# A two-block transformer kernel on one core: the first block's two norms taken out of the products, x loaded in column pieces

## The chip, the cores and the metric

The kernel runs on one core of a Trainium2 chip. The metric is the device time of one execution in microseconds (us); 3 runs of the kernel before gave a median of 2947.12 us. The engines are named as in the profile: PE (TensorE, the matmuls), PEld (its weight loads), DVE (VectorE), ACT (ScalarE), POOL (GpSimd) and SP, which only issues transfers. Each has an instruction queue of its own that is worked off in order, and they wait for each other through semaphores.

## What is computed

Two transformer blocks on one sequence of 256 tokens with 2048 features, all in float32. The change concerns the first block, which is, cut to what matters:

```python
def rmsnorm(x, g):
    y = x * lax.rsqrt(jnp.mean(x * x, axis=-1, keepdims=True) + EPS)   # the row factor
    return y * g                                                       # the gain

h = rmsnorm(x, norm_mix)
qa, ka, va, qb, kb, vb, ga, gb = jnp.split(h @ w_in, split_points, axis=-1)
qa, ka = rope(rmsnorm(qa, a_q_norm), pos), rope(rmsnorm(ka, a_k_norm), pos)
qb, kb = rmsnorm(qb, b_q_norm), rmsnorm(kb, b_k_norm)
merged = (sigmoid(ga) * (window_attention(qa, ka, va, sink) @ w_branch_a)
          + sigmoid(gb) * (neighbourhood_attention(qb, kb, vb, rpb) @ w_branch_b))
x = x + merged @ w_out
u = rmsnorm(x, norm_ffn) @ w_up          # 2 x 5632 columns
u = depthwise_conv3(u, conv_w) + conv_b  # over tokens
gate, val = jnp.split(u, 2, axis=-1)
x = x + (silu(gate) * val) @ w_down
```

The second block (gated linear attention, spatial gating, a SwiGLU ffn, all modulated by vectors that are products with `w_mod`) has norms of its own, written with the same helpers.

## The kernel before

**Chunks.** All large products of a stage are cut into groups of 512 output columns, and a group into chunks of 512 input features. The weights of a chunk are 1 MB; SP loads them as two transfers of 512 KB into a ring of 4 slots (`load`, L444), each when the chunk 4 places before has released its slot. The stages follow one another in one numbering of chunks: projection (`proj`, 9 groups of 4 chunks), gate (8 of 4), branch (8 of 2), wout (4 of 4), up (22 of 4), down (4 of 11), and then the second block's.

**Seven products for eight.** A chunk is computed with a scheme of seven half-size products in place of eight. For this DVE forms sums of the weight quarters (`step`, L940 to L945: `step(n)` prepares chunk n + 2) and, once per norm or per input, sums of the quarters of the activations (`combine`, L973 to L978, 4 feature tiles at a time; its semaphores are called `forms_...`). PE runs the seven products twice in a chunk (L512), into PSUM banks 0 to 6. At a group's end ACT copies one of the products (`first_keep`, L1522) and DVE puts the results together (`gather`, L957 to L967).

**A norm.** `part_ss` receives sums of squares by row from ACT (`sum_squares`, L1532; for the ffn norm `squares_of_x`, L1658), POOL makes the row factor `norm_rs` of them (`rows_rstd`, L1908 to L1916), DVE multiplies x by it, 256 columns at a time (`norm_tok`, L985), PE turns the result into feature-major form (`norm_piece`, L530; a norm has 8 such pieces of two feature tiles), ACT multiplies each tile by its gain on the way out of PSUM into `act_t` (`norm_keep`, L1543), and DVE combines. PE calls `norm_ahead` in the first three chunks: pieces 0 to 3 before chunk 0, 4 and 5 before chunk 1, 6 and 7 before chunk 2.

**The start.** SP loads the upper 128 rows of x and ACT the lower ones (1 MB each); SP's first weight load waits for the latter. ACT loads the identity matrix and the gains, waits for x, squares it, issues the 21 loads of constants (L1564) and only then comes to `norm_keep`. POOL, after the row factor and chunk 0, issues two loads of `w_mod`, 8 small ones of the bias table, and the `skew` write (L1956), which lays that table out in memory with a shift for each row.

**Head work.** In the projection, the heads of a group are normed while the next group runs: DVE gathers it in the next group's chunk 0, ACT squares it, DVE reduces (`head_squares`), ACT takes the root (`head_rstd`), DVE scales it in chunk 1 (`head_first`, L1071) and, for the rotated heads, does `head_second` in chunk 2 (L1089 to L1092); PE turns two heads behind chunk 3 (L544). The turns go through bank 7, whose users take it in an order worked out beforehand (`BANK7`).

**The modulation.** The second block's modulation vectors are accumulated all along the first block, a half (512 KB of `w_mod`, loaded by POOL, L1940) at a time, on DVE (L1035), at the chunks that `HALVES` names; `SUMS_AFTER` says behind which chunk PE turns a finished sum (L554).

**Wout to up.** After wout's last group DVE adds it to x (`wout_add`, L1176), ACT squares the last 512 columns, POOL makes the factor, and the ffn norm starts as above. In up, group 2i holds gate columns and 2i + 1 value columns. Each is gathered into `up_g` or `up_v`, turned by PE after the second following chunk (L562), and convolved by ACT and DVE.

## Time and profile before

| | |
|---|---|
| three runs | 2945.26, 2947.12, 2952.03 us |
| the profiled execution | 2944.24 us, its span 2942.4 us |
| PE busy | 2858.7 us, 97% of the span |
| PEld busy | 2405.0 us, 82% |
| DVE busy | 1957.8 us, 67% |
| ACT busy | 413.7 us, 14% |
| POOL busy | 346.8 us, 12% |
| mean granted clock of TensorE | 0.993 of 2.4 GHz |
| memory traffic | 569.47 MB, 194 GB/s over the span |

The span goes from the first to the last instruction; the execution's time is somewhat longer. The busy shares are means over stages that differ, so they say which engine works most and not what a wait is worth. For that one has to see at each place which wait ended last. Times in the timeline are from the span's start.

### The profile page before, as it was taken

The numbers are of one execution on the slowest core, as the hardware profiler recorded it, in microseconds if no ns is written. First come the engines' busy times: TensorE is split into PE (matmuls) and PEld (weight loads), VectorE is DVE, ScalarE is ACT, GpSimd is POOL, SyncE is SP. The second block draws the span as 40 slices with busy tenths as digits, with TensorE's granted clock in tenths as the row PEclk, the third lists the DMA queues.
The fourth block names the chain that finished last, engine by engine and source line by source line (L and its number), as shares of the span: only waits on it lengthen the run. The fifth ranks groups of instructions, "written<-read, shape, count | busy, mean of one in ns | idle before, by whom it ended". The sixth has DMA issues, their size and how long they took to land.

```text
span 2942.4 us, 34314 instructions
## 1 busy us (share of the span) xinstructions
PE 2858.7 (97%) x13116; PEld 2405.0 (82%) x13116; DVE 1957.8 (67%) x3074; ACT 413.7 (14%) x899; POOL 346.8 (12%) x428
## 2 busy tenths in 40 slices
PE   6999999998999999999999999999799999999998
PEld 5888888887888888888884467778688888888887
DVE  4887777987988898888761003348676666555454
ACT  2221112011111111110012122331200000000000
POOL 1011221010112121210110001111011111010000
PEclk9999999999999999999999999999999999999999
DMA  7677666676666666677773444437576676555553
GB/s 229 184 254 233 191 193 195 213 247 191 210 206 201 207 207 207 207 245 243 251 235 110 135 135 137 124 120 225 162 222 214 212 213 207 171 171 164 173 176 123
DMA packets 269765, 569.47 MB, mean 194 GB/s; under 512 B 20330, under 2 KB 21240, under 8 KB 269088
## 3 DMA queue, kind: packets, MB, share of 16 engines
q1 hardware_dynamic: 235728, 456.19, 50.1%
q0 software_dynamic: 30416, 108.87, 12.0%
q10 hardware_dynamic: 3456, 2.21, 0.3%
q8 instruction: 104, 1.70, 0.2%
q14 instruction: 61, 0.50, 0.0%
HBM read 563.28 MB, written 3.92 MB: 193 GB/s over the span
## 4 chain that ended last, share of the span: by engine, by line
PE 69%; issue 17%; DVE 6%; DVEq 3%; DMA 2%; ACT 1%; ACTq 0%; POOL 0%; POOLq 0%
PE PS L512 53%; PE PS L695 7%; PE PS L705 4%; DVEq L942 1%; DVE mem L1035 1%; DVE sums L943 1%; DVE sums L940 1%; DVE sums L945 1%; PE PS L562 1%; DMA mem<-in_w_mod 1%; DVE ring L941 1%; PE PS L842 1%; PE PS L530 0%; PE PS L715 0%; PE PS L554 0%
## 5 line engine op out<-in xcount | busy, mean ns | idle before, releaser
L512 PE MATMUL PS<-sums,mem 128*128 128x256 f32 x3584 | 1066.9, 379 | 0.0
L512 PE MATMUL PS<-ring,mem 128*128 128x256 f32 x3152 | 893.6, 379 | 0.0
L512 PE MATMUL PS<-ring,act_t 128*128 128x256 f32 x2928 | 794.2, 380 | 3.6 <-DVE mem L978 2.4
L512 PEld LDWEIGHTS PS<-sums,mem 128*128 128x128 f32 x3584 | 681.7, 190 | 93.0
L512 PEld LDWEIGHTS PS<-ring,mem 128*128 128x128 f32 x3152 | 596.1, 190 | 79.5
L512 PEld LDWEIGHTS PS<-ring,act_t 128*128 128x128 f32 x2928 | 548.9, 191 | 75.2 <-DVE mem L978 3.3
L940 DVE TENSOR_TENSOR sums<-ring 128x512 f32<-128x512 f32 x380 | 277.5, 730 | 394.0 <-PE PS L512 363.6
L1035 DVE SCALAR_TENSOR_TENSOR mem<-mem,small 128x512 f32<-128x512 f32 x480 | 353.0, 756 | 36.8 <-DMA mem<-in_w_mod 7.4
L1940 POOL DMA_DIRECT2D mem<-in_w_mod x192 | 139.3, 726 | 1599.7 <-DVE mem L1035 1481.4
L943 DVE TENSOR_TENSOR sums<-sums,ring 128x512 f32<-128x512 f32 x380 | 276.7, 728 | 29.5 <-issue 1.3
L945 DVE TENSOR_TENSOR sums<-sums,ring 128x512 f32<-128x512 f32 x380 | 270.8, 713 | 30.0 <-issue 2.2
L512 PE MATMUL PS<-sums,act_t 128*128 128x256 f32 x976 | 290.3, 379 | 0.0
L941 DVE TENSOR_TENSOR ring<-ring 128x512 f32<-128x512 f32 x380 | 260.4, 685 | 0.0
L512 PEld LDWEIGHTS PS<-sums,act_t 128*128 128x128 f32 x976 | 185.7, 190 | 25.3
L705 PE MATMUL PS<-mem,ring 128*128 128x256 f32 x640 | 142.7, 382 | 0.0
L695 PE MATMUL PS<-ring,mem 128*128 128x512 f32 x320 | 139.3, 592 | 0.0
L1522 ACT COPY first_q<-PS 128x256 f32<-128x256 f32 x85 | 31.7, 373 | 756.4 <-PE PS L512 756.4
L705 PEld LDWEIGHTS PS<-mem,ring 128*128 128x128 f32 x640 | 121.7, 192 | 17.5 <-issue 1.2
L695 PEld LDWEIGHTS PS<-ring,mem 128*128 128x128 f32 x320 | 60.1, 190 | 70.9 <-issue 70.8
L1681 ACT ACTIVATE mem<-PS,small 128x256 f32<-128x256 f32 x88 | 44.9, 561 | 375.9 <-PE PS L562 375.9
L957 DVE TENSOR_TENSOR mem<-PS,first_q 128x512 f32<-128x512 f32 x85 | 58.1, 684 | 52.6 <-PE PS L512 52.0
L1277 DVE SCALAR_TENSOR_TENSOR mem<-PS,mem 128x2048 f32<-128x2048 f32 x2 | 4.6, 2291 | 124.7 <-ACT mem L1741 124.7
(242 smaller groups left out, 1631.8 us busy)
## 6 DMA issues: line engine op xcount, KB each, us to landing
ring<-in_w_in SPq DMA_DIRECT2D x240, 512.0 KB, 3.7
mem<-in_w_mod POOLq DMA_DIRECT2D x192, 512.0 KB, 4.9
ring<-in_w_up SPq DMA_DIRECT2D x176, 512.0 KB, 3.8
ring<-in_w_ffn_in SPq DMA_DIRECT2D x176, 512.0 KB, 3.7
ring<-in_w_down SPq DMA_DIRECT2D x88, 512.0 KB, 4.3
ring<-in_w_ffn_out SPq DMA_DIRECT2D x88, 512.0 KB, 3.8
ring<-in_w_out SPq DMA_DIRECT2D x64, 512.0 KB, 4.5
ring<-in_w_branch_a SPq DMA_DIRECT2D x16, 512.0 KB, 3.6
```

Source lines behind the costliest of these rows:

```text
L512: mm = pe.matmul(product(g, j), of(j, 2 * (c if part is None else part) + q), weights(j, n, q), start=lead and j in OPENS, stop=tail, skip ...
L695: mm = pe.matmul(PS[:, bank + h, :], act_[:, CK * c + k, h * P:(h + 1) * P], ring[:, n % SLOTS, k // 2, k % 2, :], start=c + k == 0, stop= ...
L705: mm = pe.matmul(PS[:, bank + f // 2, (f % 2) * T:(f % 2) * T + T], ring[:, n % SLOTS, k // 2, k % 2, f * P:(f + 1) * P], act_[:, CK * c + ...
L940: ve.tensor_tensor(to[:, 0], b11, b12, ADD)
L941: ve.tensor_tensor(b12, b22, b12, ADD)
L943: ve.tensor_tensor(to[:, 1], to[:, 0], b22, ADD)
L945: ve.tensor_tensor(to[:, 2], to[:, 1], b21, ADD).then_inc(s["sums_ready"], 1)
L957: ve.tensor_tensor(both(c11, c12), two(Q2), bc(first_q[:, g % 2].unsqueeze(1), [P, 2, 256]), ADD)\
L1035: op = ve.scalar_tensor_tensor(acc[:, which, :], wm[:, h % 2, k, :], col, acc[:, which, :], MUL, ADD)
L1522: act.copy(first_q[:, g % 2], product(g, Q1)).then_inc(s["first_kept"], 1)
L1681: op = act.activation(dst[:, 2 * part + f, :], PS[:, 7, f * T:(f + 1) * T], ACT.Identity, scale=conv[:, k, 1:2], bias=conv[:, k, 3:4])
L1940: pool.dma_start(wm[:, h % 2], w_mod[:, kt:kt + 2, col:col + CN]).then_inc(wm_loaded[h % 2], 16)
```

## The change

The row factor multiplies whole rows, so that it can be applied to the products' results instead of to x. The two norms of the first block now turn x itself, with the gain alone, and the factor is applied later: to the heads' squares and their factor, to v, inside the sigmoids of the gates, and to each gathered group of up. x comes in four pieces of 512 columns, all rows each, on SP's queue, the first two ahead of the first weights; the constants move to SP's queue behind chunk 3's weights. The ffn norm's pieces are turned inside wout, through bank 7. Some buffers move to other places (`up_g`, `up_v`, `ext_f`, `conv_v`, `ctx_tok`), the loads of the second block's context move back on POOL's queue, and the modulation has one half more in the projection and one less in wout. The diff, without the parts that only rename or move buffers:

```diff
-for _k in range(12, 36):
+for _k in range(11, 36):
     HALVES[N0["proj"] + _k] = 1
...
-for _k in range(16):
+for _k in range(15):
     HALVES[N0["wout"] + _k] = 1
...
-            _late = 4 if N0["gate"] <= _n < N0["branch"] else 3 if _n < N0["wout"] else 2
+            _late = 4 if _n < N0["gate"] else 5 if _n < N0["up"] else 2
...
+    _p = _n - N0["wout"]
+    if 4 <= _p < 16 and _p % 4 in (1, 2):
+        BANK7.append(("ffn", 2 * (_p // 4) + _p % 4 - 3))
+    if _p in (16, 17):
+        BANK7.append(("ffn", _p - 10))
...
-            sp.dma_start(x_tok[:, 0, :], a["x"][0:P, :]).then_inc(s["x0_loaded"], 16)
-            sp.wait_ge(s["x1_loaded"], 16)
+            def load_x(n):
+                cols_ = slice(CN * n, CN * (n + 1))
+                sp.dma_start(x_tok[:, :, cols_], a["x"].rearrange("(h p) d -> p h d", p=P)[:, :, cols_])\
+                    .then_inc(x_loaded[n], 16)
+
+            load_x(0)
+            load_x(1)
             for g in range(9):
                 for c in range(4):
                     load(N0["proj"] + 4 * g + c, w_in, CK * c, CN * g)
+                    if g == 0 and c < 2:
+                        load_x(2 + c)
+                    if (g, c) == (0, 3):
+                        for dst, src in consts:
+                            sp.dma_start(dst, src).then_inc(s["consts_loaded"], 16)
...
             def norm_piece(key, j, src):
+
                 n = norm_sems[key]
-                pe.wait_ge(n["tok"], j + 1)
-                if key == "ctx":
-                    bank7_take("ctx", j)
+                if key == "mix":
+                    pe.wait_ge(x_loaded[j // 2], 16)
+                elif key == "ffn":
+                    pe.wait_ge(s["wout_added"], j // 2 + 1)
+                else:
+                    pe.wait_ge(n["tok"], j + 1)
+                if key in ("ctx", "ffn"):
+                    bank7_take(key, j)
                 elif j >= 2:
                     pe.wait_ge(n["kept"], j - 1)
...
                     chunk(n, G0["wout"] + g, c, 4, of_m)
                     if g == 0 and c < 2:
                         turn_merged(3, c)
+                    if g and c in (1, 2):
+                        norm_piece("ffn", 2 * g + c - 3, None)
                     mod_sums(n)
...
                     if i == 0 and j < 4:
-                        norm_ahead("ffn", j, ffn_tmp)
                         pe.wait_ge(s["forms_ffn"], j + 1)
                     chunk(n, G0["up"] + 2 * i + j // 4, j % 4, 4, of_f)
+                    if i == 0 and j < 2:
+                        norm_piece("ffn", 6 + j, None)
...
                     if j in (5, 6):
-                        kept_all(pe, G0["up"] + 2 * i)
+                        pe.wait_ge(s["up_scaled"], 2 * i + 1)
                         turn_tokens(("up_gate", i, j - 5), up_g, j - 5)
...
             ve.memset(d_t[2 * RANK:2 * RANK + 1, :], 1.0)
-            ve.wait_ge(s["x0_loaded"], 16)
-            ve.wait_ge(s["x1_loaded"], 16)
-            ve.wait_ge(s["first_loaded"], 32)
+            norm_combine("mix", 0, ext_x, "forms_mix")
             step(-2)
-            norm_open("mix", mix_tmp, ext_x, "forms_mix")
+            norm_combine("mix", 1, ext_x, "forms_mix")
+            step(-1)
...
-                rstd = rs[:, 0:2 * heads].rearrange("p (h n) -> p h n", h=2).unsqueeze(3)
+                rstd = rs[:, 0:2 * heads].rearrange("p (h n) -> p h n", h=2)
+                ve.tensor_tensor(rstd, rstd, bc(norm_rs.unsqueeze(2), [P, 2, heads]), MUL)
+                ve.drain()
+                rstd = rstd.unsqueeze(3)
...
                     if g and c == 0:
                         wout_add(g - 1)
+                    if g and c == 3:
+                        norm_combine("ffn", g - 1, ext_f, "forms_ffn")
                     mod_halves(n)
             wout_add(3)
...
-            act.dma_start(x_tok[:, 1, :], a["x"][P:T, :]).then_inc(s["x1_loaded"], 16)
             for dst, src in first:
                 act.dma_start(dst, src).then_inc(s["first_loaded"], 16)
             act.wait_ge(s["setup_done"], 1)
-            sum_squares("mix", x_tok, mix_junk, ready=lambda h, part: act.wait_ge(s[f"x{h}_loaded"], 16))
-            for dst, src in consts:
-                act.dma_start(dst, src).then_inc(s["consts_loaded"], 16)
             act.wait_ge(s["first_loaded"], 32)
-            for j in range(8):
-                norm_keep("mix", j, act_t, g_mix)
+
+            def squares_of_x(g, to):
+                for h in range(2):
+                    act.activation(to, x_tok[:, h, CN * g:CN * (g + 1)], ACT.Square,
+                                   accum_out=part_ss[:, 2 * g + h:2 * g + h + 1])
+                    act.drain()
+
+            for g in range(4):
+                for j in (2 * g, 2 * g + 1):
+                    norm_keep("mix", j, act_t, g_mix)
+                squares_of_x(g, mix_junk)
+            act.drain().then_inc(norm_sems["mix"]["squared"], 1)
             act.wait_ge(s["consts_loaded"], 16 * N_CONSTS)
             act.activation(c_vec, c_vec, ACT.Silu).then_inc(s["c_ready"], 1)
+            act.wait_ge(norm_sems["mix"]["rstd"], 1)
...
-                act.activation(gates[:, g], gates[:, g], ACT.Sigmoid)
-                act.activation(gates[:, 4 + g], gates[:, 4 + g], ACT.Sigmoid).then_inc(s["gates_squashed"], 1)
+                for k in (g, 4 + g):
+                    for h in range(2):
+                        op = act.activation(gates[:, k, h, :], gates[:, k, h, :], ACT.Sigmoid,
+                                            scale=norm_rs[:, h:h + 1])
+                op.then_inc(s["gates_squashed"], 1)
...
-            for j in range(4):
-                norm_keep("ffn", j, act_t, g_ffn)
+
+            def up_scale(g, buf):
+                kept_all(act, G0["up"] + g)
+                for h in range(2):
+                    op = act.activation(buf[:, h, :], buf[:, h, :], ACT.Copy, scale=norm_rs[:, h:h + 1])
+                op.then_inc(s["up_scaled"], 1)
...
+                    if i and j == 0:
+                        up_scale(2 * i - 1, up_v)
                     if j == 3:
                         first_keep(G0["up"] + 2 * i)
+                    if j == 4:
+                        if i == 0:
+                            act.wait_ge(norm_sems["ffn"]["rstd"], 1)
+                        up_scale(2 * i, up_g)
...
-            norm_rstd("mix")
+            norm_rstd("mix", 4)
             pool.wait_ge(s["weight_used"], 2)
...
-            pool.wait_ge(s["weight_used"], 2 * N0["down"])
-            for h in range(2):
-                pool.dma_start(ctx_tok[:, h, :], a["ctx_2"][h * P:(h + 1) * P, :]).then_inc(s["ctx_loaded"], 16)
             mod_loads(2)
...
             combine(*pairs_of(10), "forms_h")
+            for h in range(2):
+                pool.dma_start(ctx_tok[:, h, :], a["ctx_2"][h * P:(h + 1) * P, :]).then_inc(s["ctx_loaded"], 16)
```

## Rows read from the trace of the kernel before

**Rows 1.** Who waited for whom, PE over the whole span: total, times, longest.

```profile
PE PS L530 <- DVE mem L985: 41.6, 3, 17.6
...
PE PS L544 <- DVE mem L1092: 2.8, 1, 2.8
...
PE PS L512 <- DVE sums L945: 1.3, 1, 1.3
```

**Rows 2.** Timeline from 0 to 60 us: start, length, instruction, idle before it.

```profile
0.74 0.39 SPq L447 DMA_DIRECT2D x_tok<-in_x  x1
...
8.55 1.28 ACT L1532 ACT_TABLE_LOAD   x1 [8.55 <-DMA x_tok<-in_x]
...
14.12 0.69 DVE L940 TENSOR_TENSOR sums<-ring 128x512 f32<-128x512 f32 x1 [13.00 <-DMA ring<-in_w_in]
...
16.86 2.19 DVE L985 TENSOR_SCALAR mem<-x_tok,small 128x256 f32<-128x256 f32 x8
...
17.62 1.94 PE L530 MATMUL PS<-ident,mem 128*128 128x128 f32 x8 [17.62 <-DVE mem L985]
...
25.83 1.57 ACT L1543 ACTIVATE act_t<-PS,small 128x256 f32<-128x256 f32 x4 [11.91 <-issue]
...
27.43 0.42 DVE L973 TENSOR_TENSOR mem<-act_t 128x256 f32<-128x256 f32 x1 [5.65 <-ACT act_t L1543]
...
48.29 1.68 POOL L1956 DMA_DIRECT2D skew<-mem  x1 [4.10 <-DMA mem<-in_b_rpb]
```

**Rows 3.** The chain that ended last, 0 to 120 us: start, length, what.

```profile
29.25 8.97 PE PS L512 x28
38.22 0.87 PE PS L530 x8
39.09 6.04 PE PS L512 x28
...
52.08 13.69 DMA ring<-in_w_in
...
86.57 1.08 PE PS L544 x4
87.65 6.91 PE PS L512 x28
```

**Rows 4.** Timeline of DVE between 60 and 96 us.

```profile
65.97 0.69 DVE L940 TENSOR_TENSOR sums<-ring 128x512 f32<-128x512 f32 x1 [10.98 <-DMA ring<-in_w_in]
...
83.83 0.69 DVE L1089 TENSOR_TENSOR mem<-mem 128x512 f32<-128x512 f32 x1
```

**Rows 5.** Timeline where wout hands over to up.

```profile
690.73 0.59 PE L512 MATMUL PS<-sums,mem 128*128 128x256 f32 x2
...
694.20 0.63 ACT L1658 ACTIVATE mem<-x_tok 128x512 f32<-128x512 f32 x1 [5.06 <-DVE x_tok L1176]
...
695.87 0.19 POOL L1908 TENSOR_TENSOR small<-small 128x4 f32<-128x4 f32 x1 [10.30 <-ACTq L1672]
...
698.80 0.72 POOL L1916 TENSOR_TENSOR small<-small 128x2 f32<-128x2 f32 x1 [0.15 <-issue]
...
700.45 1.97 PE L530 MATMUL PS<-ident,mem 128*128 128x128 f32 x8 [9.13 <-DVE mem L985]
...
705.14 1.13 PE L512 MATMUL PS<-ring,act_t 128*128 128x256 f32 x4 [0.96 <-DVE mem L978]
```

**Rows 6.** Weight loads L444 until 100 us; all transfers until 21 us in 40 slices.

```profile
DMA to landing us min/median/max: 3.5/4.9/13.7
...
GB/s 0 0 0 187 78 250 312 437 437 406 453 437 421 406 267 46 0 0 55 109 261 382 429 386 429 382 421 390 386 406 382 382 382 375 384 369 378 373 369 346
```

**Rows 7.** Windows: one projection group, one wout group; clock, DMA share, GB/s last.

```profile
143.00:168.00 25.00, 25.00 (x119) 22.03 (x118) 21.61 (x32) 5.20 (x7) 2.89 (x4) 1.00 0.80 256
642.60:667.20 24.60, 24.60 (x118) 21.66 (x116) 19.81 (x29) 3.03 (x13) 2.84 (x4) 1.00 0.77 256
```

## What I expect, before any run

> **What bounds the kernel now.** I began with who kept TensorE (PE) waiting, because PE is busy for 97% of the span: a microsecond counts only if PE stood still in it, ran slowly, or has less to do afterwards. All idle time of note comes from three waits on L985, the row scaling of the norms, 41.6 us together, the longest 17.6; then two waits in the projection, 2.8 and 1.3 us [rows 1]. The second view, the timeline of the start, shows what lies behind the 17.6 us [rows 2]. The third, the chain that ended last, gives the length of a chunk and of what is slow [rows 3]; the fourth is the middle of the projection [rows 4]; the fifth the hand-over from the output projection (wout) to up, with the second L985 wait [rows 5]. The third L985 wait belongs to the second block, which the change doesn't touch. Last come the loads [rows 6] and how full VectorE (DVE) is, since it gets work in new places [rows 7].
>
> At the start the reader should see a serial chain: x issued at 0.74 and landed at 8.55; ScalarE's (ACT) table load and two squares; POOL's row factor; DVE scales x from 16.86; PE transposes at 17.62; and then ACT, which alone can keep the turned tiles, starts at 25.83, because it was issuing 21 constant loads (its 11.91 us of idle time has the releaser "issue") [rows 2]. The first chunk starts at 29.25. A chunk takes 6.04 us, the first one 8.97: its first matmuls run at about half speed, 2.9 us lost [rows 3].
>
> At wout to up PE's last matmul ends at 691.32, its transposes begin at 700.45, slow again, and up's first chunk starts at 705.14. In between: the add to x until 694.20, squares until 695.87, POOL's factor until 699.5, L985, transposes, keeps, combination [rows 5].
>
> **The start.** From the path go the factor, half of x's loading, the weight loads' wait for x, and the constants on ACT's queue. SP's queue now holds x's column piece 0 (512 KB), piece 1, then chunk 0's weights (two of 512 KB); ACT's the identity and the gains. Step by step:
> - Piece 0 lands. Loads of 512 KB took 3.5 us at least and 4.9 in the middle [rows 6]; nothing is ahead of this one, so I take 3.7: 4.45. The upper bound is x as it is now, 7.8 us.
> - A column piece is turned as two tile pairs of 4 transposes. Slow, 8 took 1.94 us; the first pair is there at 5.5. ACT's table load still comes, 1.28: 6.8. It keeps two pairs in 1.57: 8.4. DVE's combination took 1.8 us, from 27.43 to PE's start at 29.25 [rows 2, 3]: 10.2.
> - Chunk 0's weights have 1 MB ahead of them. The 2 MB of x took 7.8 us, and pieces of 512 KB in a row ran at 370 to 430 GB/s in most slices [rows 6], so they land at about 8.8, before DVE wants them at 10.2.
> - DVE's sums of the weights take 2.8 (14.12 to 16.86 [rows 2]): 13.0. With the hops between, chunk 0 starts at 13.2 in place of 29.25: **16.0 us off**.
>
> The slow first matmuls stay at 2.9 us; they could cost nothing, or all of chunk 0 could be slow (12.1 us, 3.1 more than now). The group has as many transposes as before. The later pieces of x are covered: 2 and 3 stand behind one and two chunks of weights, land at about 10 and 14, and are wanted after chunk 0 (22) and chunk 1 (29). ACT now squares 512 columns at a time between the keeps, 1.67 us a pair (694.20 to 695.87 [rows 5]); the first pair delays the keeps of column piece 1 to 12, its combination to 15 and DVE's sums of chunk 1 to 18.2, still before chunk 0 ends. The constants' 21 issues stand on SP's queue behind four chunks of weights, from about 6 to 18 us; queued behind them is chunk 4's load, wanted at 33. Nothing there is late.
>
> One rule speaks against cutting x. Queued pieces of 512 KB moved here at the full rate, one behind another [rows 6]. The Trainium skill ("DMA: Bandwidth & Descriptors", Bandwidth) asks for batches of at least 1 MiB and prices one transfer at 2.0 us plus its bytes over 436 GB/s; were that paid anew for each of the four pieces up to chunk 0's weights, an estimate from that page, they would land at 13.6, chunk 0 would start at 16.4 and the whole sum would be 28.4 instead of 31.6.
>
> **The middle of the projection.** Today a slow write collides with the weights: POOL's skew write is issued at 48.29, 10.1 us after chunk 0's end at 38.22; a load issued at 52.08 then takes 13.7 us [rows 2, 3]; DVE sits until 65.97, everything behind it is late, and PE waits 1.3 and 2.8 us [rows 1, 4]. After the second wait PE is slow: 1.08 and 6.91 us for a turn and a chunk that take 0.44 (half of 0.87) and 6.04, 1.5 more [rows 3]. So 5.6 us are lost. After the change POOL's queue first waits for the factor in four parts: the last squares come after the transposes behind chunk 1 (29) and ACT's keeps, at 33; the factor at 36.5 (3.65 us, 695.87 to 699.5 [rows 5]). The modulation and bias loads queued behind it take the same 10 us, so the skew write goes at 46.5 and lasts to about 63, while chunk 4 runs from 42. Now it is chunk 8's load, issued by 48, that lands at about 62, where it was chunk 6's. The gather of group 0 and the first half of its head work are done by then; what queues behind the load on DVE is chunk 8's sums (until 65) and the second half, 2.7 us (83.83 to 86.57 [rows 3, 4]). PE wants its turn at 66.2 and gets it at 67.7: 1.5 us of idle. Saved: 4.1, or 2.6 if PE slows down again. Bounds: all 5.6, or nothing. I take **3.5**, nearer to the case without a slow spell.
>
> Elsewhere in projection and gate: a product that puts the row factor into the head factor (a small one on DVE, at most the 0.7 us of a full one [rows 2], 7 times), one more modulation half at chunk 11, squares split in two, v and the sigmoids scaled by row. DVE is busy 21.6 of 25 us there [rows 7], and PE waits for nothing after chunk 8 [rows 1]: zero. Without that cover the seven products would cost up to 5 us.
>
> **Wout to up.** Six of the eight tile pairs are now turned behind wout's chunks through bank 7, the last two behind up's chunks 0 and 1. Up's chunk 0 needs only what was ready inside wout and starts at 691.32, not 705.14: 13.8. The transposes of four pairs, 0.44 each, were inside that gap and are now outside it: minus 1.7. **12.1 off.** DVE gets three combinations of 1.8 in wout and one modulation half less; it is busy 19.81 of a group's 24.6 us [rows 7], so there is room. The last pairs need the last add, done by 694.20; PE comes for them at 697.4. Behind, ACT scales each up group: weight sums 2.8, gather at most 2.9 (691.32 to 694.20), scale 1.3 (two of 0.63 [rows 5]), 7.0 us after the group ends; PE turns it after two more chunks, 12.1. Slack 5, cost zero. The context loads move from the head of down to behind the last gating; they are wanted a group later. Zero.
>
> Sum: 16.0 + 3.5 + 12.1 = 31.6 us. The profiled execution took 2944.24 us around its span of 2942.4; the median of the runs is 2947.12, 2.9 above it. All three terms lie inside the span, so they come off the median as well: 2947.1 - 31.6 = **2915.5**.
>
> **The rivals.**
> 1. Column piece 0 lands with the rest, since all transfers share the engines: at 8.5, and chunk 0 starts at 17.0. Saves 27.8: 2919.3. For it: x landed at 8.55 although each half was issued by itself. Against: both halves were in flight together on two queues; now they stand in one.
> 2. The skew write meets the weights no better, or PE slows down again on top: term two is 0, 2919.0. For it: my chain leaves 1.5 us of idle, and 3 us more delay of chunk 8's load fills the difference.
> 3. DVE becomes the bound in wout. With 19.81 + 1.8 of 24.6 it must first lose 3 us a group to waits; at 2 us more in each of three groups, 2921.5.
> 4. The change doesn't do what it says at up: the pairs' turn at bank 7 holds PE inside wout, and half of term three stays: 2921.5.
> 5. Slower: the row scale stands between gather and turn for all 22 up groups. About 5 us each is hidden, then PE waits. To cancel 31.6 us it must run 1.4 us over in each, a scale of 7.8 us in place of 1.3; at 8.5 us the time is 2962. No row speaks for it.
>
> **How the numbers follow.** Forecast 0.55, rivals 0.10, 0.15, 0.08, 0.06 and 0.02; 0.04 remain for more than 5 us better. The forecast's own unknowns (slow first chunk -2.9 to +3.1, the middle +2.1 or -3.5, piece 0, spread of runs 2) give 2910 to 2920; rivals 1 to 4 reach 2924 with them. Range 2909 to 2924. A measurement tells a change from none at 0.2%, 5.9 us: every case but the fifth, or a heap of several, is faster by more. Faster 0.96, same 0.02, slower 0.02.
>
> **What would show it.** First chunk at about 13; under 2 us of idle at the first head turn; none between wout's last and up's first chunk; no wait of PE on up's turns. Wrong if chunk 0 starts after 17, if DVE's sums release PE in wout, or if PE waits on ACT's scaling.

## The result, and the profile after

The changed kernel takes **2916.88 us** (median of 4 runs, 2913.17 to 2920.41), the kernel before beside it on the same chip 2946.19 us (4 runs). The ratio is 0.9897, 95% interval [0.9878, 0.9916]: 29.3 us, or 1.0%, faster. The forecast was 2915.5 us with a range of 2909 to 2924. The profiled execution took 2916.29 us.

Line numbers have moved: L528 is the matmul of a chunk (L512 before), L556 the turn of a norm's pieces (L530), L569 the turn of heads (L544), L968 to L973 the sums of weights (L940 to L945), L1001 to L1006 the combination (L973 to L978), L1574 the keep (L1543), L587 the turn of a group of up (L562).

First the head of the page after, then who kept PE waiting over the whole span (total, times, longest):

```profile
span 2914.4 us, 34383 instructions
...
PE 2858.8 (98%) x13116; PEld 2404.8 (83%) x13116; DVE 1950.7 (67%) x3049; ACT 451.1 (15%) x975; POOL 347.2 (12%) x430
```

```profile
PE PS L556 <- DVE mem L1013: 14.8, 1, 14.8
PE PS L556 <- DMA small<-in_norm_mix: 6.1, 1, 6.1
...
PE PS L528 <- DVE sums L973: 3.3, 1, 3.3
...
PE PS L569 <- DVE mem L1123: 1.9, 1, 1.9
```

The three waits on the row scaling, 41.6 us in [rows 1], have become one: the 14.8 us that is left is the second block's norm, which the change does not touch. In the first block stand two long waits at the start, on the load of the gains (6.1) and on the weight sums of chunk 0 (3.3), and one of 1.9 us at the first head turn, where [rows 1] had 2.8 and 1.3; its other waits are of 1.5 us or less.

**The start.** The timeline after, 0 to 50 us (start, length, instruction, idle before it):

```profile
1.20 0.45 ACTq L1590 DMA_DIRECT2D small<-in_norm_mix  x1
...
6.06 1.97 PE L556 MATMUL PS<-ident,x_tok 128*128 128x128 f32 x8 [6.06 <-DMA small<-in_norm_mix]
...
7.29 1.28 ACT L1574 ACT_TABLE_LOAD   x1 [7.29 <-PE PS L556]
8.58 1.57 ACT L1574 ACTIVATE act_t<-PS,small 128x256 f32<-128x256 f32 x4
...
10.18 0.43 DVE L1001 TENSOR_TENSOR mem<-act_t 128x256 f32<-128x256 f32 x1 [9.06 <-ACT act_t L1574]
...
11.86 0.69 DVE L968 TENSOR_TENSOR sums<-ring 128x512 f32<-128x512 f32 x1
...
14.83 2.04 PE L528 MATMUL PS<-ring,act_t 128*128 128x256 f32 x4 [3.32 <-DVE sums L973]
...
24.43 25.66 SPq L450 DMA_DIRECT2D ring<-in_w_in  x10
```

Compare with [rows 2]: no factor, no square and no scaling stands ahead of the transposes, and ACT comes to its keeps at 8.58, where it came at 25.83. What released PE at 6.06 is not x. The median of the four x loads is 7.8 us from issue to landing, but the first landed 4.3 us after its issue, at 5.04; the 8 KB of gains, issued at 1.20, landed at 6.02. Chunk 0's weights are not the releaser either: their two loads landed at 8.77 and 10.58, and DVE's first weight sum at 11.86 shows no idle time, it follows straight on the combination. The constants' issues on SP's queue run from 11.30 to 24.38, and chunk 4's load goes out at 24.43, after chunk 0 has ended.

The chain that ended last, after, from 0 to 130 us (start, length, what):

```profile
1.20 4.82 DMA small<-in_norm_mix
...
14.83 8.94 PE PS L528 x28
23.77 0.87 PE PS L556 x8
24.64 6.05 PE PS L528 x28
...
49.73 14.47 DMA ring<-in_w_in
...
68.32 1.24 DVE mem L1123
...
69.69 0.63 PE PS L569 x4
70.32 6.04 PE PS L528 x28
76.36 0.44 PE PS L569 x4
```

Beside [rows 3]: chunk 0 starts at 14.83 (29.25), chunk 1 at 24.64 (39.09): 14.4 us earlier. The skew write still meets the weights. POOL issued it at 46.86, and it took 17.1 us; the load issued at 49.73 took 14.47 us, and PE comes to the first head turn 1.9 us before the heads are ready. But it is a later load of the ring than before, and behind the wait PE is hardly slowed down: the turn takes 0.63 us, 0.2 more than the next one, and the chunk 6.04, not 6.91.

**Wout to up.** The same chain between 640 and 720 us:

```profile
669.62 6.04 PE PS L528 x28
675.67 0.44 PE PS L579 x4
676.10 6.05 PE PS L528 x28
...
688.63 0.44 PE PS L556 x4
689.07 24.18 PE PS L528 x112
```

Up's chunk 0 is the one at 676.10, straight behind wout's last chunk. PE idles nowhere from 560 to 720, where it idled from 691.32 to 700.45 and again before 705.14 in [rows 5].

The window of a group of wout, which answers to the second of [rows 7] (columns: the window and its length, then busy time and instructions of PE, PEld, DVE, ACT, POOL, granted clock, DMA share, GB/s), and below it ACT's scale of the first up group in the timeline:

```profile
624.45:649.05 24.60, 24.60 (x120) 21.66 (x119) 20.86 (x33) 3.38 (x9) 2.84 (x4) 1.00 0.76 254
```

```profile
706.86 1.34 ACT L1731 ACTIVATE mem<-mem,small 128x512 f32<-128x512 f32 x2 [7.88 <-DVE mem L995]
```

DVE in a group of wout is busy 20.86 of 24.6 us (19.81 before): the combinations found room. The scale ends at 708.20, and PE turns this group at 713.25 (the chain): 5.05 us of cover are left.

**Where the 28.0 us of span were gained, by the place in the program.** Each is the difference of the two chains, before minus after, at the same instruction.

| at | before | after | earlier by | added since the place above |
|---|---|---|---|---|
| chunk 0 | 29.25 | 14.83 | 14.42 | 14.4 |
| turn behind the chunk after the first head turn | 94.56 | 76.36 | 18.20 | 3.8 |
| up, chunk 2 | 719.67 | 689.07 | 30.60 | 12.4 |
| second block's ffn norm, first transposes | 2109.75 | 2079.89 | 29.86 | -0.7 |
| the same norm, before its second chunk | 2121.05 | 2093.06 | 27.99 | -1.9 |
| end of the span | 2942.4 | 2914.4 | 28.0 | 0.0 |

The three parts add to 30.6 us; 2.6 are given back in the second block, whose code and work are the same. There the chains of the two kernels read, before first:

```profile
2109.75 1.13 PE PS L530 x4
...
2114.74 6.31 PE PS L512 x28
```

```profile
2079.89 1.13 PE PS L556 x4
...
2084.88 8.18 PE PS L528 x28
```

The same first chunk takes 6.31 us in one and 8.18 in the other. The window around it, 2080 to 2100 us after, has a granted clock of 0.78:

```profile
2080.00:2100.00 20.00, 18.97 (x82) 15.96 (x83) 13.43 (x34) 5.79 (x12) 0.00 (x0) 0.78 0.36 105
```

In the records of the granted clock TensorE is at its lower level (1.2 GHz) from 2099.7 for 13.7 us before, and from 2068.2 for 20.5 us after. Both begin inside PE's wait of 15 us for the second block's ffn norm. The one before ends at 2113.4, ahead of the first chunk; the one after ends at 2088.7, 3.8 us into it.

### The profile page after: what moved, and what is told of

Same layout as the page of the kernel before. It is cut to its first block, busy times and chain, and to the rows that moved or that the text cites. A ratio compares the mean times of both kernels' runs of the same rounds, so it can differ in the third digit from the quotient of the medians.

```text
span 2914.4 us, 34383 instructions
## 1 busy us (share of the span) xinstructions
PE 2858.8 (98%) x13116; PEld 2404.8 (83%) x13116; DVE 1950.7 (67%) x3049; ACT 451.1 (15%) x975; POOL 347.2 (12%) x430
## 3 DMA queue, kind: packets, MB, share of 16 engines
q0 software_dynamic: 30416, 108.87, 12.1%
## 4 chain that ended last, share of the span: by engine, by line
PE 73%; issue 17%; DVE 5%; DVEq 2%; DMA 1%; ACT 1%; POOL 0%; POOLq 0%; ACTq 0%
PE PS L528 56%; PE PS L723 7%; PE PS L733 4%; DVEq L970 1%; DVE sums L971 1%; DVE mem L1064 1%; DVE sums L968 1%; PE PS L587 1%; DMA mem<-in_w_mod 1%; DVE sums L973 1%; PE PS L556 1%; PE PS L870 1%; DMA ring<-in_w_in 0%; PE PS L743 0%; PE PS L579 0%
## 5 line engine op out<-in xcount | busy, mean ns | idle before, releaser
L528 PE MATMUL PS<-sums,mem 128*128 128x256 f32 x3584 | 1068.2, 380 | 0.0
L528 PE MATMUL PS<-ring,mem 128*128 128x256 f32 x3152 | 894.7, 380 | 0.0
L528 PE MATMUL PS<-ring,act_t 128*128 128x256 f32 x2928 | 794.5, 380 | 3.9 <-DVE sums L973 3.3
L528 PEld LDWEIGHTS PS<-sums,mem 128*128 128x128 f32 x3584 | 682.7, 190 | 93.3
L528 PEld LDWEIGHTS PS<-ring,mem 128*128 128x128 f32 x3152 | 596.2, 190 | 79.4
L528 PEld LDWEIGHTS PS<-ring,act_t 128*128 128x128 f32 x2928 | 549.3, 191 | 75.1 <-issue 3.7
L968 DVE TENSOR_TENSOR sums<-ring 128x512 f32<-128x512 f32 x380 | 276.5, 728 | 376.1 <-PE PS L528 356.8
L528 PE MATMUL PS<-sums,act_t 128*128 128x256 f32 x976 | 290.4, 379 | 0.0
L973 DVE TENSOR_TENSOR sums<-sums,ring 128x512 f32<-128x512 f32 x380 | 270.8, 713 | 28.2
L528 PEld LDWEIGHTS PS<-sums,act_t 128*128 128x128 f32 x976 | 185.7, 190 | 25.3
L1553 ACT COPY first_q<-PS 128x256 f32<-128x256 f32 x85 | 31.6, 372 | 717.3 <-PE PS L528 717.3
L723 PE MATMUL PS<-ring,act_t 128*128 128x512 f32 x192 | 85.5, 603 | 0.0
```

What stands on the lines that cost most here:

```text
L528: mm = pe.matmul(product(g, j), of(j, 2 * (c if part is None else part) + q), weights(j, n, q), start=lead and j in OPENS, stop=tail, skip ...
L723: mm = pe.matmul(PS[:, bank + h, :], act_[:, CK * c + k, h * P:(h + 1) * P], ring[:, n % SLOTS, k // 2, k % 2, :], start=c + k == 0, stop= ...
L968: ve.tensor_tensor(to[:, 0], b11, b12, ADD)
L973: ve.tensor_tensor(to[:, 2], to[:, 1], b21, ADD).then_inc(s["sums_ready"], 1)
L1553: act.copy(first_q[:, g % 2], product(g, Q1)).then_inc(s["first_kept"], 1)
```

## The experiments

The medians of the kernel before beside these runs were 2947.28, 2946.74 and 2946.82 us. The theory is the prediction's: three gains that add, each made by the step that it names. The rivals are in the expectations.

### The two halves apart

e1_mix_only takes the changed kernel and puts the ffn norm back as it was; e2_ffn_only takes the kernel before and adds the ffn half alone. The core of e1's edit:

```diff
-                elif key == "ffn":
-                    pe.wait_ge(s["wout_added"], j // 2 + 1)
...
-                    if g and c in (1, 2):
-                        norm_piece("ffn", 2 * g + c - 3, None)
...
-                pe.wait_ge(s["up_scaled"], 2 * i + 2)
+                kept_all(pe, G0["up"] + 2 * i + 1)
...
+                        norm_ahead("ffn", j, ffn_tmp)
...
+            norm_open("ffn", ffn_tmp, ext_f, "forms_ffn")
```

> The change without its ffn half: x's norm, the column pieces, the constants on SP's queue and the row factor applied to heads, v and gates stay; the ffn norm scales x, turns and keeps it before up as in the kernel before. Theory (two separate gains that add): the start and the middle of the projection give what they give in the whole change, 14.4 and 3.8 us, so 18.2 us less than before, 2928, and the gap between wout and up is back at 13.8 us. Rival (the ffn half carries the gain, since the start is paid back in the projection): within 5 us of before, 2942 to 2947. Rival (part of the loss in the second block comes from the new ffn part): more than 18.2 us are saved here, 2925.

> The other half alone: the kernel before with the ffn norm turned inside wout through bank 7, and each up group scaled by row after its gather; the start is as before. Theory: 13.8 us of gap less 1.7 of transposes, 12.1 us saved, 2934; VectorE busy about 21 of 24.6 us in a wout group and no wait of PE there. Rival (bank 7 or VectorE holds PE in wout): 4 us or more of new waits of PE between the start of wout and up, 2938 or above.

e1: 2929.98 us, ratio 0.9944 [0.9929, 0.9959]. e2: 2934.45 us, 0.9961 [0.9946, 0.9976]. Against the kernel before, 17.3 and 12.8 us: together 30.1, about the whole. The halves don't hide each other, and the split is close to the prediction's (16.0 + 3.5, and 12.1), the start's miss included. In e2 the start and the middle of the projection are those of before: chunk 0 at 29.34, waits of 2.1 and 1.1 us in the middle. In e1 the gains landed 6.42 us after their issue; chunk 0 came at 16.43, chunk 1 at 25.76.

### What the start consists of

e3_consts_only is the kernel before with the 21 loads of constants issued by SP behind chunk 3's weights in place of ACT; nothing else.

```diff
-            for dst, src in consts:
-                act.dma_start(dst, src).then_inc(s["consts_loaded"], 16)
...
+                    if (g, c) == (0, 3):
+                        for dst, src in consts:
+                            sp.dma_start(dst, src).then_inc(s["consts_loaded"], 16)
```

> The kernel before with one edit: the 21 loads of constants are issued by SP behind chunk 3's weights and no longer by ACT. Theory (ACT's 11.9 us of issuing were the last thing that the first chunk waited for, the row factor only the next): the first keep follows the first transposes at 18.7, the combination ends at 22.1, chunk 0 starts at about 22.2, 7 us saved, 2939; the row factor is worth only the rest of the start. Rival (the row factor is what counted): chunk 0 stays within 2 us of 29.25, and the time within 2 us of before.

2941.96 us, ratio 0.9982 [0.9973, 0.9992]; its chain:

```profile
23.26 8.00 PE PS L515 x28
...
32.13 6.05 PE PS L515 x28
```

Chunk 0 comes 6.0 us earlier than in [rows 3] and is 1 us shorter, so that chunk 1 comes 7.0 us earlier. That is about half of the 14.45 us at chunk 1 in the changed kernel: half of the start's gain has nothing to do with the row factor, it is ACT's queue set free. The whole time falls by 5.3 us (6.5 in the profiled spans), where 7 was expected: behind the wait between wout and up the first chunk takes 7.85 us here, not 6.31.

e4_x_rows is the changed kernel with x loaded as two row halves of 1 MB instead of four column pieces of 512 KB:

```diff
-                sp.dma_start(x_tok[:, :, cols_], a["x"].rearrange("(h p) d -> p h d", p=P)[:, :, cols_])\
-                    .then_inc(x_loaded[n], 16)
+                sp.dma_start(x_tok[:, n, :], a["x"][P * n:P * (n + 1), :]).then_inc(x_loaded[0], 16)
...
-                    pe.wait_ge(x_loaded[j // 2], 16)
+                    pe.wait_ge(x_loaded[0], 32)
```

> The changed kernel with x loaded as two pieces of 128 rows (1 MB each), both ahead of the first weights on SP's queue, in place of four column pieces; everything else stays. Theory (queued pieces move one behind another at the full rate, so the cut lets the first transposes go early): PE's first transposes wait for x until about 8.5 instead of 6.06, chunk 0 starts 2.5 us later at 17.3, 2919.5. Rival (the first transposes are held by the small loads and the end of chunk 0's path by its weights, so that x's pieces hardly matter): chunk 0 within 1 us of 14.8, 2917. Rival (each 512 KB piece pays a fixed price): chunk 0's weights land earlier here and it starts before 14.8.

2918.78 us, 0.9905 [0.9889, 0.9922]. Its chain:

```profile
1.17 7.51 DMA small<-in_norm_mix
...
17.48 7.86 PE PS L524 x28
...
26.21 6.05 PE PS L524 x28
```

Chunk 0 came where expected (17.3), 2.65 us later than in the changed kernel, but it ran in 7.86 us, not 8.94, so that at chunk 1 only 1.57 us of the difference are left. The slower half of x landed 7.3 us after its issue, at about 8.5, the gains at 8.68, so the row halves hold the start to about the same point with the gains out of the way. The time doesn't settle it: 2 us are within the runs' spread. Nor does chunk 1. Three further profiles have the start of the changed kernel without any edit to it (e11, e7 and e8, below): their chunk 0 begins at 16.17, 16.23 and 16.25, their chunk 1 at 24.83, 25.89 and 26.32. Against them e4 is 1.2 to 1.3 us later at chunk 0, and at chunk 1 (26.21) it lies among them. What is left of the start, 14.45 - 7.0 - 1.6 = 5.9 us at chunk 1, is the factor's part with the new order of x and weights; it is a difference of single profiles, not a run of its own, and rough by as much as chunk 1 varies, 1.7 us.

### The gains' load, the last to land

e5_ident_wait lets PE wait for the identity alone and only ACT for the gains:

```diff
-            act.wait_ge(s["first_loaded"], 32)
+            act.wait_ge(s["gain_loaded"], 16)
...
-            pe.wait_ge(s["first_loaded"], 32)
+            pe.wait_ge(s["first_loaded"], 16)
```

> The changed kernel; PE waits for the identity alone, and ACT for the gain, each through its own semaphore. In the changed kernel PE's first transposes are released at 6.06 by the gain's load, while the identity had landed at 3.8 and x's piece 0 at 5.04. Theory (the start's chain is as the prediction had it, shifted by that one load): transposes at 5.1, chunk 0 at about 13.9 in place of 14.83, 0.9 us less at chunk 0. From the runs before: PE reached full speed at about 20.5 whenever it began early, so a start 1 us earlier may add up to 0.5 us of slow matmuls, and 0.4 to 0.9 us are left at chunk 1, 2916. Rival (ACT's first keep still waits for the gain): less than 0.3 us at chunk 0.

2917.18 us, 0.9904 [0.989, 0.9919]. PE began at 5.2, but nothing followed:

```profile
1.22 6.30 DMA small<-in_norm_mix
...
15.12 9.22 PE PS L528 x28
```

The gains landed at 7.52, and ACT's table load with the first keep waits for them: that much of the rival held. Chunk 0 at 15.12 looks like its number too, but the gains landed 1.5 us later than in the profile of the changed kernel. From their landing to chunk 0 it took 7.6 us here, against 8.8 in the changed kernel, in e4 and in e11. So PE's wait for the gains does cost 1.2 us at chunk 0, about what the theory had, because the turn no longer stands behind it; at chunk 1 (25.22) and in the whole time nothing of it shows.

e9_gain_first puts the gains' load first on SP's queue, ahead of x; ACT issues the identity alone:

```diff
+            sp.dma_start(*first[1]).then_inc(s["first_loaded"], 16)
             load_x(0)
             load_x(1)
...
-            for dst, src in first:
-                act.dma_start(dst, src).then_inc(s["first_loaded"], 16)
+            act.dma_start(*first[0]).then_inc(s["first_loaded"], 16)
```

> The changed kernel with the gain's 8 KB load issued by SP ahead of x's pieces; ACT issues the identity alone. In the runs so far that load, issued at 1.2 behind the identity and beside x, landed only at 6.0 to 7.6, and it held the first transposes or (where PE didn't wait for it) the first keep. Theory (the small load is late because x's large ones are in flight before it): it lands before x's piece 0, so PE starts when that lands, about 5.3, and chunk 0 starts at 14.1, and at 14.1 in every such run; chunk 1 starts at 24.0 to 24.6, since full speed comes at 20 to 21 in all runs. 2916, at most 1 us less than the changed kernel. Rival (128 rows of 64 bytes take that long wherever they stand): PE starts at 6 to 7.5 again.

2916.47 us, 0.9898 [0.9881, 0.9914]. The same 8 KB now landed in 2.1 us, and x is what PE waits for:

```profile
1.18 4.23 DMA x_tok<-in_x
...
5.55 1.10 PE PS L557 x4
...
14.28 8.81 PE PS L529 x28
...
23.97 6.04 PE PS L529 x28
```

PE starts 0.5 us earlier than in the changed kernel, chunk 0 0.55 and chunk 1 0.67 us. That the gains' load is what held PE's start is shown; that it is worth something in the whole time is not, 0.4 us are less than can be told.

### The skew write

e6_skew_early issues the loads of the bias table at once and the skew write right behind chunk 0, ahead of the row factor on POOL's queue:

```diff
-            norm_rstd("mix", 4)
-            pool.wait_ge(s["weight_used"], 2)
-            mod_loads(2)
...
             pool.wait_ge(s["rpb_loaded"], 128)
+            pool.wait_ge(s["weight_used"], 2)
             src = bc(rpb[:, 0:P - 1].unsqueeze(1), [56, GRID, P - 1])
             pool.dma_start(skew.rearrange("r (q c) -> r q c", c=P)[:, :, 0:P - 1], src).then_inc(s["skew_written"], 16)
+            norm_rstd("mix", 4)
+            mod_loads(2)
```

> The changed kernel; POOL issues the small bias loads at once and the skew write right after chunk 0, and makes the norm's row factor only after that. In the changed kernel the skew write is issued at 46.5, the load of 49.73 takes 14.5 us, and PE waits 1.9 us for the second half of the head work. Theory (what costs is that the collision meets a DVE queue with head work behind the late load): the write now runs from about 25 to 42, the loads of chunks 4 and 5 are late, but chunk 4's sums are wanted only at 43.6 and no head work is queued behind them; PE's wait of 1.9 and the 0.2 of slow transposes go, 2 us saved, 2915. Rival (the collision costs wherever it is): PE waits for chunk 4's or chunk 5's sums for 2 us or more, no gain or a loss, and the sum of waits before 100 us doesn't fall.

2916.82 us, 0.9902 [0.9886, 0.9919]. The write was issued at 24.75 and took 17.0 us; the wait at the first head turn is gone, and a new one of 0.3 us stands at 44.29 (PE for the first copied product, whose ACT waited for POOL's factor). From the first matmul of chunk 1 to the head turn at 118.81 (119.98 in the changed kernel) it took 94.0 us against 95.5. So the write's place is the cause of the 1.9 us wait, as the prediction had it; the time doesn't tell it from the changed kernel.

e10_start_all has e9's and e6's edits and an early activation that brings ACT's table load ahead of x's landing:

```diff
             act.wait_ge(s["setup_done"], 1)
+            act.activation(gate_col[:, 0:1], one_col, ACT.Identity)
             act.wait_ge(s["first_loaded"], 32)
```

> The gain first, the skew write early as in the run before, and one small activation on ACT ahead of its wait, so that the table load (1.28 us) happens while x is under way. Theory (the three lie on the chain one after another): PE starts at 5.3, the first keep at 6.5, chunk 0 at 12.8, chunk 1 at about 23.3 (slow until 20), no wait in the middle: against the changed kernel 1.3 at chunk 1 and 2.1 in the middle, 3.4 us, 2913.5. Rival (chunk 0's weights are the next bound): chunk 0 not before 13.8, released by the load. Rival (slow matmuls eat all of an earlier start): chunk 1 still at 24.6, 2 us in all.

2917.8 us, 0.99 [0.9885, 0.9915]: a miss. The start is the best of all:

```profile
13.20 7.95 PE PS L529 x28
...
25.78 15.41 DMA ring<-in_w_in
...
44.10 16.07 PE PS L529 x66
```

Chunk 1 at 22.02 is 2.6 us ahead of the changed kernel. But the weight load issued at 25.78 took 15.41 us beside the write, as the one at 49.73 does in the changed kernel, and here it is chunk 4's. DVE's sums of it end at 44.06 and PE waits 3.1 us for them, with TensorE slow again behind the wait. By the chunk after the first head turn all that the start had gained is gone. In e6 the same early write cost 0.3 us, because chunk 4's two loads went out at 24.23 and 24.71, just ahead of it. Here chunk 0 ends at 21.15 and POOL writes at 21.83, but SP is still issuing constants until 24.10, so that chunk 4's loads, at 24.15 and 25.78, fall behind the write. So the write costs by what is queued behind it on the ring, and it was the constants on SP's queue that put this load there. With the constants elsewhere it was not tried.

### The scale of up, made longer

The prediction's only losing case was the row scale between gather and turn. e7_scale_x4 and e8_scale_x7 repeat ACT's two scaling passes 3 and 6 more times in each of the 22 up groups, into a spare buffer:

```diff
                 kept_all(act, G0["up"] + g)
+                for _ in range(3):
+                    for h in range(2):
+                        act.activation(spare[:, h, :], buf[:, h, :], ACT.Copy, scale=norm_rs[:, h:h + 1])
+                    act.drain()
```

> The changed kernel with ACT's row scale of each up group made four times as long: three more passes over the group into an unused buffer ahead of the real one (nothing of the result changes). In the changed kernel a group ends at 701.2, its gather at 706.8, its scale at 708.2, and PE turns it at 713.3, so 5.1 us are hidden; three passes of 1.34 us and their drains take 4.3. Theory: still hidden, within 3 us of the changed kernel. Rival (the scale is already on the path, or ACT's other work behind it has no slack): 4.3 us in each of 22 groups, up to 95 us more.

> The same with six more passes, 8.7 us. Theory (5.1 us of cover, then PE waits): PE waits 3.6 us at each of 22 turns, about 79 us, 2996, with the waits of PE's up turns (the helper for all token turns) released by ACT. Rival (the next groups' work absorbs it): less than 20 us more.

e7: 2927.84 us, 0.9941 [0.9926, 0.9956], 11 us over the changed kernel, where at most 3 were expected. The first up group in its timeline of ACT, and its waits of PE:

```profile
708.04 4.14 ACT L1733 ACTIVATE mem<-mem,small 128x512 f32<-128x512 f32 x6 [7.89 <-DVE mem L996]
712.25 1.33 ACT L1736 ACTIVATE mem<-mem,small 128x512 f32<-128x512 f32 x2
```

```profile
PE PS L588 <- ACT mem L1736: 13.8, 10, 1.7
```

The passes end at 713.58, and PE turns the group at 714.41: here 0.8 us to spare, with 4.2 us added. In 10 of the 22 turns PE waited, up to 1.7 us. So the cover is 5 us where I had worked it out, and down to 2.5 in the worst group (4.2 - 1.7).

e8: 3049.43 us, 1.0352 [1.0331, 1.0373]; expected was 2996. Its waits of PE, its window 800 to 1000 us, and then that window of the changed kernel:

```profile
PE PS L588 <- ACT mem L1736: 70.2, 17, 4.9
PE PS L588 <- ACT PS L1587: 18.6, 5, 3.7
```

```profile
800.00:1000.00 200.00, 173.12 (x776) 148.98 (x774) 144.65 (x232) 85.64 (x154) 28.52 (x28) 0.94 0.56 168
```

```profile
800.00:1000.00 200.00, 198.30 (x955) 173.93 (x954) 178.53 (x282) 37.87 (x90) 36.40 (x35) 1.00 0.68 206
```

All 22 turns wait, 88.8 us together, 4.0 each: the 8.4 us added less a mean cover of 4.4. But the time rose by 132.6 us. The difference lies in the clock: 0.94 against 1.00 in that window, TensorE running slowly for a while behind each wait. Its records show 22 spells at the lower level in up, one at the end of each wait, 92.1 us together; at half speed they cost up to 46 us, and 88.8 + 46 = 135. A wait of 4 us here cost 6. In e7, with waits of 1.7 us and less, the records show no such spell in up, and 13.8 us of waits cost 11.

### The changed kernel once more

> The changed kernel once more, unchanged. In its first profile the shift against the kernel before was 30.6 us behind the third chunk of up and 28.0 us at the end; 2.6 us were lost in the second block, whose code is the same, where TensorE's half-clock spells sum to 27.3 us against 17.1. Theory (how long these spells last is chance of when they begin, not work): another sum of spells here, between 14 and 35, and a time that goes with the mean granted clock, about 2913 at 0.995 and 2920 at 0.992. Rival (they belong to the new order of the work): the same spells at the same places, 27.3 us again.

e11_after_again is the changed kernel, unedited: 2917.37 us, 0.9899 [0.9884, 0.9914]. Its chain at the start:

```profile
16.17 7.79 PE PS L528 x28
...
24.83 6.04 PE PS L528 x28
```

The gains took 6.14 us this time, chunk 0 began at 16.17 in place of 14.83, and chunk 1 at 24.83 in place of 24.64. With e7 and e8, whose edit lies in up, there are four profiles of this start: chunk 0 at 14.83, 16.17, 16.23 and 16.25, chunk 1 at 24.64, 24.83, 25.89 and 26.32. Its slow spells after 1400 us sum to 27.3 us, as in the profile above. The two short ones lie at other places (1514.3 and 1664.5, where they stood at 1539.2 and 1962.4), the one of 20.5 us at the same (2070.6, 2068.2 above). So neither the theory's other sum nor the rival's same places came; and an execution at a mean clock of 0.995 took 2916.06 us, where the theory had 2913.

## Why the prediction was right

**The start: forecast 16.0 us, measured 14.4.** The mechanism is as it was put. The term that was mis-sized is the first, "I take 3.7: 4.45" for piece 0 to land. Piece 0 landed at 5.04, and I took the 8 KB of gains, issued behind the identity, to be there before it; they came at 6.02. Everything behind runs to the forecast's lengths: 6.06 to 10.18 for turn, table load and keeps (forecast 3.95, measured 4.1), then 1.7 for the combination (1.8) and 3.0 for the weight sums with their hops (2.8). The slow first chunk stayed at 8.94, as taken. e9 and e5 show the cause from both sides: gains first, and x is the releaser; PE freed from them, and ACT waits for them. That the miss is only 1.6 us is partly luck: in e11, e7 and e8 the gains landed at 7.4, chunk 0 began 13.0 us earlier than before, and chunk 1 12.8 to 14.3 (14.4 in the first profile).

**The pieces of x.** Rival 1 did not come: piece 0 did not land with the rest at 8.5. The Trainium skill's price of one transfer ("DMA: Bandwidth & Descriptors", Anatomy of one DMA — SWDGE (gpsimd) path), taken four times in a row, put the weights at 13.6 and chunk 0 at 16.4; it is a fit for transfers that GpSimd issues, and these are SP's. The trace disagrees: the fourth load landed at 10.58, and DVE did not wait for it. That is 1.8 us later than my 8.8 all the same, and later than the 10.2 at which my chain wanted it; with everything ahead of it on time it would have held chunk 0. The batches of 1 MiB that the same page of the Trainium skill advises (Bandwidth) are e4's. They were 1.2 to 2.65 us later at chunk 0 than the four profiles of the changed start; at chunk 1 and in the time no run here tells them apart.

**The middle of the projection: forecast 3.5, measured 3.8.** The write at 46.9 (forecast 46.5), its load landing at 64.2 (62), PE's wait 1.9 (1.5), and no slow chunk behind it. The load landed 2 us later than forecast; PE too came later, since chunk 0 had. e6 shows that the wait comes from the write's place. Rival 2 did not come. Of the 3.8, the 1.5 us of slow turn and chunk before may not be there in every execution: e3 waits 2.8 and 1.5 us at the same places, and its chunk behind them takes 6.05. Two details missed without effect: the constants' issues on SP's queue ran until 24.4, not 18, and chunk 4's load, "wanted at 33", went out at 24.43. In e10 they were no longer without effect.

**Wout to up: forecast 12.1, measured 12.4**, and 12.8 with e2 alone in the whole time. PE idles neither in wout (rival 3: DVE has 3.7 us a group left; rival 4: no turn at bank 7 holds PE) nor on up's scaling (rival 5). e7 and e8 show that rival 5's mechanism is real and where it begins: but it was under-priced. I had it break even at a scale of 7.8 us. By e8, 88.8 us of waits cost 132.6, since TensorE runs slowly behind them; with the uneven cover of e7 a scale of 5.5 us already costs 11. Linearly between e7 (5.5 us, +11) and e8 (9.7 us, +132.6), 31.6 us are lost at 6.2; with 1.5 us lost for each of wait in 22 groups beyond e8's mean cover it is 6.7. Both are estimates. The measured scale of 1.34 us is far below.

**What was not foreseen** is the 2.6 us lost in the second block, in code that is the same. They lie in spells at the lower clock level. The sum of such spells after 1400 us (without the one at the very end) was 17.1 us before and in e3, 23.9 to 27.3 in e1, e2, e5, e6, e9, the changed kernel and e11, and 34.1 in e4, e7, e8 and e10. They vary from one execution to the next: three executions of the changed kernel took 2913.17, 2916.29 and 2920.41 us at mean granted clocks of 0.995, 0.994 and 0.992. But before and e3, where both norms are still as they were, have the least, and none of the eleven profiles with at least one norm changed has less than 23.9; e2, whose start is the old one, has 27.3, so the earlier start is not what it takes. I can't say whether the change makes such a spell likelier or whether the profiles of before and e3 were lucky ones. That stays open. In the span the parts give 31.6 - 1.6 + 0.3 + 0.3 - 2.6 = 28.0. The medians differ by 30.2, since the profiled execution of before lay 2.9 us below the median shown and that of after 0.6 below; that is why the forecast misses by 1.4 us and not by 3.6. This closeness is luck: against the kernel before measured beside it, at 2946.19, the gain is 29.3 us, 2.3 short of the forecast's 31.6.

No version tried is distinguishably faster than the changed kernel: e9 by 0.4 us and e6 by 0.1 are noise.

## What to carry to other kernels

Look at what an engine's queue holds besides its work: half of this start's gain was 21 small loads taken off the queue of the one engine that could empty PSUM. When all large terms at a start have been moved, the last to land is often a tiny load issued beside large ones; issue it first, and read the releaser, not the size. What is moved to another queue can do harm there: in e10 the same loads kept chunk 4's weights behind a slow write. Work added between a product and its turn is free only up to the smallest cover of all the groups. Past that point waits of up to 1.7 us cost no more than themselves (e7), and waits of 4 us about one and a half times that (e8), because TensorE runs slowly behind them. And one profile of each kernel is not enough for a microsecond at the start: with the same code there, chunk 0 moved by 1.4 us and chunk 1 by 1.7.

## What the runs showed of the hardware that was not expected

- A load of 8 KB issued second on one queue beside large loads on another took 4.8 to 7.5 us to land in eight profiles of the changed start; issued first, 2.1 us (e9, e10).
- At the start the first record of the upper level (2.4 GHz) stands at 19.2 to 22.2 us in after, e1, e4 to e9 and e11, whose transposes begin at 5.2 to 8.7 and whose chunk 0 begins at 14.3 to 17.5; the pairs of matmuls go from 1.06 to 0.59 us there. It is not a fixed time: e3 has it at 21.0 (transposes 17.4, chunk 0 at 23.3), before and e2 at 34.7 and 34.8 (17.6, 29.3), and e10 at 9.8. In the first group a chunk 0 that begins later can make up for it (8.94 us from 14.83, 7.79 from 16.17, 7.86 from 17.48), but need not (8.78 and 9.20 from 16.2 in e7 and e8). In e3 and e10 another slow spell of 3.4 us followed (24.4 and 13.2).
- The skew write, 1778 KB, takes 16.4 to 17.3 us in all thirteen profiles, wherever it is issued, and the slowest 512 KB load behind it 12.6 us in e6 and 13.7 to 15.4 in the others, against 4.9 in the middle of the loads of [rows 6].
- TensorE's spells at the lower level sum to 17 to 34 us after 1400 us in kernels whose work there is the same. Executions of the changed kernel lie up to 7 us apart, longer mostly at a lower mean granted clock (0.995 to 0.992). In e8 22 such spells in up went with 22 waits of 4 us; in e7, whose waits are 1.7 us at most, there were none.
